# Where weight blocks lie in SBUF, modulo 128 bytes, in a two-block transformer kernel

## The reference, cut to what matters

```python
def swiglu(x, w_gate, w_up, w_down):
    return (jax.nn.silu(x @ w_gate) * (x @ w_up)) @ w_down      # D_MODEL = 1024, D_FF = 2816

proj = x @ w_in                                                  # the gated mixer
...
q = (h @ w_q)...;  k, v = jnp.split(mem @ w_kv, 2, axis=-1)      # attention over the memory
for e in range(N_EXPERTS):                                       # D_FF_EXPERT = 3584
    out = out + gates[:, e:e + 1] * swiglu(t, e_gate[e], e_up[e], e_down[e])
```

## The kernel before, in words

| moving | stationary | their places modulo 128 | modulo 256 |
|---|---|---|---|
| weights, 512 columns | `x` | 64 and 0 | 64 and 128 |
| weights, 512 columns | `cat`, `mem`, `hT` | 64 and 64 | 64 and 64 |
| `x`, 256 columns | weights | 0 and 64 | 128 and 64 |
| `mem`, 256 columns | weights | 64 and 64 | 64 and 64 |
| expert weights | `expert_in0`, `expert_in1` | 64 and 0 | |
| expert weights | `expert_in2` | 64 and 64 | 64 and 64 |

## Time and profile before

### The profile page before, as it was taken

One profiled execution on the slowest core, in us unless ns is written; L12 is line 12 of the kernel. 1 busy time (PEld: TensorE's weight loads), 2 busy tenths in 40 slices (PEclk: granted clock), 3 DMA queues, 4 the chain that ended last, 5 costly groups with the idle time before them and its releaser, 6 DMA issues.

```text
span 2598.5 us, 40653 instructions
## 1 busy us (share of the span) xinstructions
PE 2542.5 (98%) x18155; PEld 1805.7 (69%) x18155; DVE 1050.7 (40%) x1488; ACT 820.6 (32%) x1138; POOL 143.4 (6%) x143
## 2 busy tenths in 40 slices
PE   8999999999999999999999999999999999899998
PEld 6799885444444444444448987797988988798897
DVE  5755562010101001010126558646546545656554
ACT  5444342010111101010123436444444434634432
POOL 2200120000000000000000001000000004300000
PEclk9999999999999999999999999999999999999999
DMA  7565468999999999999985543446556546254651
GB/s 256 199 207 183 159 209 328 371 363 386 377 359 372 391 376 358 377 379 368 375 298 169 195 142 134 146 147 210 195 163 205 184 161 243 79 199 162 219 182 53
DMA packets 335286, 641.51 MB, mean 247 GB/s; under 512 B 15620, under 2 KB 128432, under 8 KB 334976
## 3 DMA queue, kind: packets, MB, share of 16 engines
q1 hardware_dynamic: 330000, 618.64, 66.8%
q0 software_dynamic: 5104, 20.20, 2.3%
HBM read 637.72 MB, written 1.05 MB: 246 GB/s over the span
## 4 chain that ended last, share of the span: by engine, by line
PE 92%; DVE 5%; ACT 1%; issue 1%; DMA 0%; POOL 0%; SPq 0%; DVEq 0%
PE bank L571 17%; PE bank L573 17%; PE bank L572 17%; PE bank L1193 15%; PE bank L1207 8%; PE bank L1240 7%; PE bank L1262 4%; DVE part_lo L546 2%; PE bank L967 1%; PE bank L1225 1%; PE bank L938 1%; PE bank L583 1%; DVE x_rows L1823 1%; PE bank L1179 1%; ACT part_hi L538 1%; DVE stats L1803 1%
## 5 line engine op out<-in xcount | busy, mean ns | idle before, releaser
L546 DVE TENSOR_TENSOR part_lo<-raw,part_hi 128x2048 fp32r<-128x2048 f32 x251 | 570.7, 2294 | 265.0 <-ACT part_hi L538 265.0
L538 ACT ACTIVATE part_hi<-raw 128x2048 fp32r<-128x2048 f32 x251 | 472.3, 1907 | 21.0 <-DMA raw<-in_mem_w_kv_dram 7.0
L571 PE MATMUL bank<-x_hi,part_hi 128*128 128x256 f32 x1440 | 405.2, 281 | 0.0
L573 PE MATMUL bank<-x_hi,part_lo 128*128 128x256 f32 x1440 | 402.1, 279 | 0.0
L572 PE MATMUL bank<-x_lo,part_hi 128*128 128x256 f32 x1440 | 401.8, 279 | 0.0
L571 PEld LDWEIGHTS bank<-x_hi,part_hi 128*128 128x128 f32 x1440 | 270.2, 188 | 3.9 <-issue 1.0
L572 PEld LDWEIGHTS bank<-x_lo,part_hi 128*128 128x128 f32 x1440 | 269.6, 187 | 3.0
L573 PEld LDWEIGHTS bank<-x_hi,part_lo 128*128 128x128 f32 x1440 | 270.7, 188 | 0.0
L571 PE MATMUL bank<-part_hi,x_hi 128*128 128x512 f32 x528 | 213.9, 405 | 1.3 <-DVE part_lo L546 0.9
L1193 PE MATMUL bank<-raw,expert_in 128*64 128x512 f32 x896 | 214.1, 598 | 0.0
L1193 PE MATMUL bank<-raw_hi,expert_in 128*64 128x512 f32 x896 | 211.3, 592 | 0.0
(11 more groups left out here) (270 smaller groups left out, 3428.3 us busy)
## 6 DMA issues: line engine op xcount, KB each, us to landing
raw<-in_exp_w_gate_dram SPq DMA_DIRECT2D x112, 512.0 KB, 6.6
raw<-in_exp_w_up_dram SPq DMA_DIRECT2D x112, 512.0 KB, 7.5
raw_hi<-in_exp_w_gate_dram SPq DMA_DIRECT2D x112, 512.0 KB, 8.3
raw_hi<-in_exp_w_up_dram SPq DMA_DIRECT2D x112, 512.0 KB, 9.1
raw<-in_exp_w_down_dram SPq DMA_DIRECT2D x56, 1024.0 KB, 12.8
raw_hi<-in_exp_w_down_dram SPq DMA_DIRECT2D x56, 1024.0 KB, 14.1
raw<-in_ffn_w_gate_dram SPq DMA_DIRECT2D x110, 512.0 KB, 4.1
raw<-in_ffn_w_up_dram SPq DMA_DIRECT2D x110, 512.0 KB, 5.4
```

What stands on the lines that cost most here:

```text
L538: p.nc.scalar.activation(p.part_hi[i][:, :], p.raw[i][:, :], ACT.Copy).then_inc(*self.rounded.step((name,)))
L546: p.nc.vector.tensor_tensor(p.part_lo[i][:, :], p.raw[i][:, :], p.part_hi[i][:, :].bitcast(F32), ALU.subtract).then_inc(*self.split.step(( ...
L571: nc.tensor.matmul(out, stat_hi, move_hi, start=start, stop=False, skip_group_check=True)
L573: return nc.tensor.matmul(out, stat_lo, move_hi, start=False, stop=stop, skip_group_check=True)
```

## The change

`x_hi` and the first slot are put on multiples of 128 bytes. A slot grows from 16384 to 16512 bytes, 64 spare bytes behind each half. Each slot gets two sets of tensors over the same bytes: index 0 lies at `x_hi`'s place modulo 128, index 1 (`turned_...`) 64 bytes off it. Each block says which set it uses: turned are the blocks that are stationary with 256 columns moving, by their number in the stage's list; all others, and the experts' half slots, use index 0. What lies behind the slots, and the arena over slots 6 to 8, now begins on a multiple of 128. Instructions, their order and their waits are the same.

```diff
+LINE = 128
+APART = 64
...
-        x_at = at[0]
+        x_at = at[0] = (at[0] + LINE - 1) // LINE * LINE
...
+        at[0] = (at[0] + LINE - 1) // LINE * LINE
         for i in range(RING):
             if i == MIX_RING:
                 arena = at[0]
-            raw_at = at[0]
-            self.raw.append(put(f"raw{i}", [P, SLOT]))
-            self.part_lo.append(over(f"part_lo{i}", [P, SLOT], F32R, raw_at))
-            self.raw_hi.append(over(f"raw_hi{i}", [P, SLOT], F32, at[0]))
-            self.part_hi.append(put(f"part_hi{i}", [P, SLOT], F32R))
+            raw_at, hi_at = at[0], at[0] + 4 * SLOT + APART
+            at[0] = hi_at + 4 * SLOT + APART
+            for name, turned in (("", 0), ("turned_", 1)):
+                at_place = lambda first: first + (x_at + turned * APART - first) % LINE
+                self.raw[turned].append(over(f"{name}raw{i}", [P, SLOT], F32, at_place(raw_at)))
+                self.part_lo[turned].append(over(f"{name}part_lo{i}", [P, SLOT], F32R, at_place(raw_at)))
+                self.raw_hi[turned].append(over(f"{name}raw_hi{i}", [P, SLOT], F32, at_place(hi_at)))
+                self.part_hi[turned].append(over(f"{name}part_hi{i}", [P, SLOT], F32R, at_place(hi_at)))
+        at[0] = (at[0] + LINE - 1) // LINE * LINE
...
-                                        + [(wo, c, kh) for kh in range(2) for c in (0, 512)])
+                                        + [(wo, c, kh) for kh in range(2) for c in (0, 512)], (4, 5))
...
-                self.plan_attention(st, [(w, c) for c in (0, 512, 1024)], wo, 15)
+                self.plan_attention(st, [(w, c) for c in (0, 512, 1024)], (), wo, 15)
...
-                self.plan_attention(st, [(w, c) for c in (2048, 2560, 0, 1024, 512, 1536)], wo, 15)
+                self.plan_attention(st, [(w, c) for c in (2048, 2560, 0, 1024, 512, 1536)], range(4, 12), wo, 15)
...
-                self.plan_attention(st, [(wkv, c) for c in range(0, 2 * D, 512)] + [(wq, 0), (wq, 512)], wo, 3)
+                self.plan_attention(st, [(wkv, c) for c in range(0, 2 * D, 512)] + [(wq, 0), (wq, 512)],
+                                    (0, 1, 2, 3, 8, 9, 10, 11), wo, 3)
...
-    def add(self, name, load):
+    def add(self, name, load, turned=False):
         self.names.append(name)
         self.load[name] = load
+        self.turned[name] = int(turned)
...
-                      for half, w in (("gate", w_gate), ("up", w_up))])
+                      for half, w in (("gate", w_gate), ("up", w_up))], by_tiles(q))
...
-        i = self.slot[name]
-        return self.p.part_hi[i], self.p.part_lo[i]
+        i, t = self.slot[name], self.turned[name]
+        return self.p.part_hi[t][i], self.p.part_lo[t][i]
```

More of the change, by code:

```diff
@@ L214, in place_memory @@
         self.att_stats = put("softmax_stats", [P, 16, 3, TT])
-        self.raw, self.part_hi, self.part_lo, self.raw_hi = [], [], [], []
+        self.raw, self.part_hi, self.part_lo, self.raw_hi = ([[], []] for _ in range(4))
+        at[0] = (at[0] + LINE - 1) // LINE * LINE
         for i in range(RING):
@@ L356, in plan_slots, with plan_attention @@
                         [st for st, stage in enumerate(self.stages) if stage[0] == "moe"])
-    def plan_attention(self, st, blocks, wo, last_head):
+    def plan_attention(self, st, blocks, turned, wo, last_head):
         n = 2 * len(blocks)
         self.ring.square_blocks(st, [(w, c, kh) for w, c in blocks for kh in range(2)]
-                                + [(wo, c, kh) for kh in range(2) for c in (0, 512)])
+                                + [(wo, c, kh) for kh in range(2) for c in (0, 512)], turned)
         self.ring.frees += [((st, i), None) for i in range(n)]
@@ L387, in __init__, with square_blocks @@
         self.slot, self.before = {}, {}
-    def add(self, name, load):
+        self.turned = {}
+    def add(self, name, load, turned=False):
         self.names.append(name)
         self.load[name] = load
-    def square_blocks(self, st, blocks):
+        self.turned[name] = int(turned)
+    def square_blocks(self, st, blocks, turned=()):
         for n, (w, col, kh) in enumerate(blocks):
             src = w[kh * 512:(kh + 1) * 512, col:col + 512].rearrange("(k p) n -> p k n", p=P)
-            self.add((st, n), [("whole", src)])
+            self.add((st, n), [("whole", src)], n in turned)
     def up(self, st, q, w_gate, w_up, col):
@@ L507, in where @@
             i, part = i
-            return (self.p.raw, self.p.raw_hi)[part][i], self.landed[i][part]
-        return self.p.raw[i], self.landed[i][0]
+            return (self.p.raw, self.p.raw_hi)[part][0][i], self.landed[i][part]
+        return self.p.raw[self.turned[name]][i], self.landed[i][0]
     def fetch(self, *names):
@@ L535, in round @@
         for name in self.whole(names):
-            i = self.slot[name]
+            i, t = self.slot[name], self.turned[name]
             p.act.wait_ge(*self.landed[i][0].at(name, self.load[name][-1][0]))
-            p.nc.scalar.activation(p.part_hi[i][:, :], p.raw[i][:, :], ACT.Copy).then_inc(*self.rounded.step((name,)))
+            p.nc.scalar.activation(p.part_hi[t][i][:, :], p.raw[t][i][:, :], ACT.Copy).then_inc(*self.rounded.step((name,)))
     def subtract(self, *names):
@@ L543, in subtract @@
         for name in self.whole(names):
-            i = self.slot[name]
+            i, t = self.slot[name], self.turned[name]
             p.dve.wait_ge(*self.rounded.at(name))
-            p.nc.vector.tensor_tensor(p.part_lo[i][:, :], p.raw[i][:, :], p.part_hi[i][:, :].bitcast(F32),
+            p.nc.vector.tensor_tensor(p.part_lo[t][i][:, :], p.raw[t][i][:, :], p.part_hi[t][i][:, :].bitcast(F32),
                                       ALU.subtract).then_inc(*self.split.step((name,)))
```

## The result

| | median us (lowest to highest) | ratio to the kernel before, 95% interval |
|---|---|---|
| before | 2594.55 (2592.56 to 3671.97) | |
| after | 2579.61 (2578.25 to 2581.09) | 0.9945 [0.9935, 0.9955] |

The change made the kernel 0.55% faster, 14.9 us between the medians. The forecast was 0.37%, 2588 us, which lies outside the interval of the ratio. One of the six executions of before took 3671.97 us, a slow one, and the ratio is formed without it. The profiled execution took 2579.98 us, beside 2599.77 before.

A forecast was written before the change was run, and what follows sets the result against it. TensorE, busy 98% of the span, bounds the kernel by matmul count times pitch. 9.5 + 0.8 = 10.3 us, of which 92% on the chain, 9.5 us, off 2597.2 gives 2588 us, 0.37% faster; range 2580 to 2601.

The forecast's parts named there:

- the prediction's own sum: TensorE's matmul pitches: at most 10.5 us won past `x` plus 0.8 us from `mem` moving.
- Past `x`, 9.5 us: 1584 matmuls of weights moving past `x`, 512 columns: 64 off becomes one place modulo 128, 6.0 ns less each.
- `x` moving, "nothing": 4320 matmuls of `x` moving past weights, 256 columns: index 1 keeps them 64 off, so 118.0 ns stays.
- `mem` moving, 0.8 us: 384 matmuls of `mem` moving past weights: one place becomes 64 off, 120.0 to 118.0 ns.
- Past `cat`, `mem`, `hT`, "nothing": 2088 matmuls of weights moving, 512 columns: these tensors move to multiples of 128 together with the weights, no gain.
- the second rival: Places in SBUF: the period is 256 bytes, not 128, so slots alternate; net +5.6 us, 2603 us; chance 0.16.
- Experts, splitting, loads, waits: Expert products stay 6.91 us; ScalarE, VectorE and DMA work gives nothing; `x_rows` waits grow from 7.7 us by under 1.
- The transposes: Some 500 lose their 64 bytes from the identity: taken as nothing, at worst 3.5 us lost.
- -5.2 and +6.9: The second rival's 512-column terms: 792 matmuls past `x` win 6.6 ns; 1044 past `hT`, `cat`, `mem` lose it.
- No row shows such a pitch: 512-column matmuls: no trace row reaches the skill's 215.8 ns, so its 28 us for `x` products did not extend the range.

The follow-up runs named there:

- kernel kept modulo 256: Kernel after, with unturned blocks, `cat`, `mem` and `hT` at `x`'s place modulo 256, turned blocks 64 bytes off: 2584.80 us, 0.9956 against before.
- `hT` 128 off: Kernel kept modulo 256, with `hT` alone moved 128 bytes off its weights: 2578.32 us, 0.9933 against before.
- the halves apart: Kernel kept modulo 256, plus a third set for down blocks: `part_lo` at `hT`'s place, `part_hi` 128 bytes off: 2573.02 us; repeated, 2574.24 us.
- two pads: Kernel before, with 128 bytes added ahead of the slots and 128 more behind them, no second tensor set: 2584.99 us, 0.9962.

## Why the prediction was right and wrong

The time, 2579.6 us, fell on the lower edge of the range of 2580 to 2601, 0.4 us under it as the numbers are written, and came there by more than the prediction's own sum allowed: that could win 11.3 us at most (10.5 + 0.8), and reached 2580 only by adding the scatter of the kernel before. 14.9 us came. The way in was right: with no instruction changed, only pitches moved, and the change in TensorE's busy time (-17.7 us) is nearly that of the span (-19.8). The steps were not all right.

- **Past `x`, 9.5 us: wrong in its reason, less than half in size.** Modulo 128 was the wrong period. In after, groups of 12 take 228.7 to 230.8 ns from even slots and 230.6 to 232.7 from odd ones, and none 226.7; the mean is 230.8, so 4.1 us came. The kernel kept modulo 256 has the 227.8 that was forecast.
- **`x` moving, "nothing": this is the step that failed, -13.8 us.** "64 off stays 64 off" took one pitch for one relation. The row of 118.0 ns showed one of two patterns, and the other, 113.5, was hardly in the trace of before: 4 of 165 series. The alternating halves of the down blocks, a side effect of the odd slot size, let 58 of the 70 series behind `hT` groups run at 113.5, 45 of them behind odd slots.
- **`mem` moving, 0.8 us:** right in direction, 1.7 us in size; half its series run at 113.5 instead of 118.
- **Past `cat`, `mem`, `hT`, "nothing": wrong by 3.5 us**, the loss that the second rival named, at half its size.
- **Experts, splitting, loads, waits: right.** The pair's up product in after:
```profile
541.76 1.94 PE L1203 MATMUL bank<-raw,expert_in 128*64 128x512 f32 x8
...
548.67 1.89 PE L1250 MATMUL bank<-raw,hT 128*64 128x512 f32 x8
```
6.91 us, as in the earlier trace rows. The waits for `x_rows` stayed 7.7 us. The chain of after has 2% on GpSimd and 1% on DMA, where before had 0: through one stretch it goes over the `bias` tiles. The sum of pitches (-16.1) is 1.2 us more than the medians show, so no cost of more than about 2 us can hide there. The transposes cost nothing that can be seen: those of `mem_row`, which went from 64 bytes off the identity to its place modulo 128, follow each other at 109 ns on average in both traces, those of `p` at a median of 109 in both.

The second rival, given 0.16, had the period, the alternation and both directions for 512 columns, but the wrong sign for the whole. It gave `x` moving in half the slots a loss of 2 ns, and all slots won, 3.2 on average. Its -5.2 and +6.9 stand beside -4.1 and +3.5 measured, and they were not reached in its way: by its rule each matmul would go by its own place, (2 x 232.4 + 226.7) / 3 = 230.5 ns in slot 2 and (232.4 + 2 x 226.7) / 3 = 228.6 in slot 3, where 229.2 and 232.5 were measured.

So it was luck that the forecast came out near: a gain of 5 us too much and a missed loss of 3.5 were covered by a missed gain of 13.8. Why I missed it: I compared one pitch for each kind, and did not go through the series of one kind for a second value. 4 of them had it.

Counts times differences give the other kernels within 4 us of what was measured: +4.3 (measured +2.9) without the turned set, -1.6 (+1.8), +6.7 (+6.7) and -11.7 (-9.3) with the slots moved by 64, 192 and 128, -12.9 (-11.4) modulo 256, -21.3 (-17.4) with `hT` 128 off, -24.6 (-21.3) with the halves apart, -11.4 (-9.9) with two pads. Measured stands for the ratio less one, times 2595.

**Open.** That what ran ahead decides the pattern is shown (same addresses, 0 or 70 of 70). Why an `hT` group sets 113.5 where `part_hi` is 128 off and `part_lo` at its place, turns the pattern over with the two the other way round or with `hT` 128 off in the kernel with two pads, and leaves 113.5 with `hT` 128 off in the kernel modulo 256, is not explained. Nor is why, with 512 columns, a slot with its halves 128 apart is slower when only `part_lo` is off. Nor is why 64 ahead and 64 behind differ, or whether the period is more than 256.

## What to carry to other kernels

Where TensorE is busy nearly all the time, measure the pitch of each kind of product by its operands' places, and compare series of one kind with each other, not only kinds: a second value in a few series can be a state that the rest may be brought into, as here. Change places in steps of 64 bytes over at least 256, one tensor group at a time, and read pitches, since gains of one kind are paid back by another (slots + 64: -9 and +9 us). Two identity matmuls can turn the pattern over as a test, but cost what they win.

## What the runs showed of the hardware

- *Stationary and moving operands of these matmuls interact by place modulo 256 bytes, or more.* With 512 columns moving, for the moving tensor's place less the stationary one's: 0 gives 226.7 ns, +64 228.9, 128 232.4, -64 233.3. With 256 columns and the weights stationary: one place 120.0, 128 off 119.6, 64 off 113.5 or 117.8, whichever side. These hold for series in which every matmul has the same difference; where it changes inside a product, as in the slots of after, a matmul's own difference does not give the pitch (229.2 ns with two of three 128 off, 232.5 with one). The full-float32 expert products don't feel it (6.91 us in both). The Trainium skill (SBUF — State Buffer, "A bandwidth-pool intuition that's wrong (but worth ruling out)") names a second, independent read port for the weight load. From that alone one would expect no effect of the operands' relative place, and these runs show one; where they meet is not shown.
- *One product, at fixed addresses, has two pitches that last.* Steps repeat as 113, 113, 114 or as 118, 118, 117 for 48 matmuls, over two slots, and the 70 series behind `hT` groups had the same pattern in both profiles of after and in both of the kernel with the down halves apart. An `hT` group of 12 or two identity matmuls turn one into the other.
- *The split (fp32r) products never reached the pitch of the full-float32 ones.* The lowest means are 226.7 and 113.3 ns at a mean granted clock of 0.995 to 0.997. The Trainium skill (TensorE: Matmul & The Clock Gate, "Wait — 56ns, not 53.3ns?") would give 215.8 and 109.2, an estimate by its columns / 2.4 GHz plus 2.5 ns; no fp32r series here reached that. The full-float32 expert products come to its figure on average: 32 matmuls of 512 columns in 6.91 us, 215.9 ns each, though they start two at a time, 0.43 us from pair to pair. So "No row shows such a pitch" in the prediction overlooks, which has this average; for the `x` products it stands.
